# Regrouping the norm between the stages of a two-block transformer kernel, and a shorter prologue

## What is computed

```
def rms_norm(x, gain):
    xf = x.astype(jnp.float32)
    y = xf * lax.rsqrt(jnp.mean(xf * xf, axis=-1, keepdims=True) + EPS)
    return (y * gain.astype(jnp.float32)).astype(x.dtype)

def modulate(x, gain, shift, scale):
    return rms_norm(x, gain) * (1.0 + scale[:, None]) + shift[:, None]

    mod = cond @ ada_w[l] + ada_b[l]
    sh1, sc1, g1, sh2, sc2, g2, sh3, sc3, g3 = jnp.split(mod, N_MOD, axis=-1)
    h = modulate(x, norm_ffn1[l], sh1, sc1)
    x = x + 0.5 * (1.0 + g1)[:, None] * swiglu(h, ffn1_w1[l], ffn1_w3[l], ffn1_w2[l])
```

## Time and profile before

| | us |
|---|---|
| three runs | 3274.8, 3290.96, 3296.43 |
| median | 3290.96 |
| the profiled execution's own time | 3291.47 |
| its span, first to last instruction | 3289.7 |

### The profile page before, as it was taken

The page is one execution under the profiler, slowest core; times in us unless marked ns, Lnnn a source line. Parts: engine busy times, 40 slices in busy tenths (PEclk is TensorE's granted clock), DMA queues, the critical chain, the costliest instruction groups (busy, mean ns, idle before and its releaser), DMA issues.

```text
span 3289.7 us, 62648 instructions
## 1 busy us (share of the span) xinstructions
PE 3056.7 (93%) x24944; PEld 2881.9 (88%) x24944; DVE 2290.9 (70%) x3886; ACT 1374.4 (42%) x2129; POOL 239.7 (7%) x315
## 2 busy tenths in 40 slices
PE   1999987999999998889999998799899999999898
PEld 1999885899999997669999998699856899999798
DVE  6887564558867675555786888587957568676654
ACT  1445413444444452243444436443644444444332
POOL 1002001010000110000101000000023100100001
PEclk9999988899999998899999999899979899999899
DMA  7895401248967651015687884287400368676253
GB/s 293 308 332 184 136 2 64 91 166 294 335 227 276 218 172 46 19 61 185 230 309 253 313 310 159 90 309 285 160 1 26 129 240 318 244 262 234 95 188 122
DMA packets 172570, 631.99 MB, mean 192 GB/s; under 512 B 19152, under 2 KB 19408, under 8 KB 171856
## 3 DMA queue, kind: packets, MB, share of 16 engines
q1 hardware_dynamic: 123696, 450.88, 38.9%
q10 hardware_dynamic: 48672, 178.28, 15.6%
HBM read 628.04 MB, written 1.05 MB: 191 GB/s over the span
## 4 chain that ended last, share of the span: by engine, by line
PE 86%; DVE 10%; ACT 2%; DMA 1%; issue 1%; POOL 0%; DVEq 0%; SPq 0%; ACTq 0%
PE psum L531 23%; PE psum L533 22%; PE psum L532 22%; DVE w_lo L503 2%; DVE xl L1830 2%; PE psum L1985 2%; PE psum L1972 1%; PE psum L549 1%; PE psum L550 1%; DMA ada_w<-ada_dram 1%; PE psum L1987 1%; PE psum L649 1%; DVE bc L1830 1%; PE psum L555 1%; PE psum L1181 1%
## 5 line engine op out<-in xcount | busy, mean ns | idle before, releaser
L531 PE MATMUL psum<-h_hi,w_hi 128*128 128x256 f32 x4464 | 1251.4, 280 | 6.1 <-DVE h_lo L1724 4.6
L533 PE MATMUL psum<-h_lo,w_hi 128*128 128x256 f32 x4464 | 1248.4, 280 | 0.0
L532 PE MATMUL psum<-h_hi,w_lo 128*128 128x256 f32 x4464 | 1247.0, 279 | 0.0
L503 DVE TENSOR_TENSOR w_lo<-raw,w_hi 128x1024 fp32r<-128x1024 f32 x852 | 1041.3, 1228 | 181.5 <-ACT w_hi L490 180.4
L490 ACT ACTIVATE w_hi<-raw 128x1024 fp32r<-128x1024 f32 x852 | 873.4, 1054 | 408.6 <-DMA raw<-stream_dram 292.3
L531 PEld LDWEIGHTS psum<-h_hi,w_hi 128*128 128x128 f32 x4464 | 840.6, 188 | 16.3 <-issue 8.4
L532 PEld LDWEIGHTS psum<-h_hi,w_lo 128*128 128x128 f32 x4464 | 840.7, 188 | 0.0
L533 PEld LDWEIGHTS psum<-h_lo,w_hi 128*128 128x128 f32 x4464 | 840.4, 188 | 0.0
L532 PE MATMUL psum<-u_hi,w_lo 128*128 128x256 f32 x1584 | 448.3, 283 | 0.0
L531 PE MATMUL psum<-u_hi,w_hi 128*128 128x256 f32 x1584 | 448.2, 283 | 0.0
L533 PE MATMUL psum<-u_lo,w_hi 128*128 128x256 f32 x1584 | 448.2, 283 | 0.0
(11 more groups left out here) (357 smaller groups left out, 3617.4 us busy)
## 6 DMA issues: line engine op xcount, KB each, us to landing
raw<-stream_dram SPq DMA_DIRECT2D x852, 512.0 KB, 4.2
ada_w<-ada_dram ACTq DMA_DIRECT2D x328, 512.0 KB, 4.7
tmp<-c_dram ACTq DMA_DIRECT2D x8, 512.0 KB, 3.4
x<-x_dram SPq DMA_DIRECT2D x1, 1024.0 KB, 12.5
ctx_x<-ctx_dram ACTq DMA_DIRECT2D x1, 1024.0 KB, 5.4
means<-means_dram ACTq DMA_DIRECT2D x1, 1024.0 KB, 5.6
out_dram<-tmp SPq DMA_DIRECT2D x1, 1024.0 KB, 3.9
const<-const_dram SPq DMA_DIRECT2D x1, 848.5 KB, 8.8
```

The costliest lines, as they stand in the source:

```text
L503: p.nc.vector.tensor_tensor(p.w_lo[:, slot].rearrange("p k m -> p (k m)"), p.raw[:, slot], p.w_hi[:, slot].rearrange("p k m -> p (k m)").b ...
L531: mm(out, p.w_hi[:, slot, k], hi, start=start, stop=False, skip_group_check=skip)
L532: mm(out, p.w_lo[:, slot, k], hi, start=False, stop=False, skip_group_check=skip)
L533: return mm(out, p.w_hi[:, slot, k], lo, start=False, stop=stop, skip_group_check=skip)
```

## The change

- **Squares.** Where the norm follows an FFN, `gates`, `ssd_out` or `state` stage, GpSimd squares x[:, 0] to x[:, 6] and adds them into one tile, `sq_sum` (7 squares and 6 sums), in tiles 4 to 6 of `tmp`, without the wait for the modulation products. DVE squares x[:, 7] itself (`last_square`). PE sums two tiles (4 products) instead of eight.
- **Root.** ACT reads the sums from PSUM, applies scale and epsilon and takes the root in one instruction; a small Sqrt without a wait stands ahead of it (`table`). DVE then takes the reciprocal. The mean on DVE is gone.
- **Order on DVE.** `prep` and the first of the two splits move ahead of the update of x[:, 7] (`lead`), the second split moves behind h_lo. Norms 9 and 14 keep both behind the last update.
- **Prologue.** 16 modulation tiles instead of 28; the gate of the first FFN is formed inside that FFN (`late_gate`), which takes 56 tiles instead of 44. `c` has a buffer of its own and the first product no longer waits for the constants. Three units are split between the products, the first norm's sums and root run beside them. SP loads three units, then waits until 13 products are done, and loads the other five; most of the constants and `par2` come behind these.
- **Rope tables.** The 22 DVE instructions for the angles (`trig_vector`) move from the start into the first `project` stage, behind the split at t = 25; the two Sin instructions of ACT into the first `gdn` stage.
- **Fetches.** The loads of `ctx` and `means` move behind the norm that they stood ahead of.
- Several semaphores are merged, which changes no wait's place.

```diff
+SQ_STEPS = 2 * (KD - 1) - 1
+HEAD_SPLITS = (9, 11, 13)
...
     for c in range(SLOTS):
+        if c == len(HEAD_SPLITS):
+            sp.wait_ge(p.sem["ada_summed"], ADA_HEAD - 3)
         load(0, c)
+    for to, src in late:
+        sp.dma_start(to, src).then_inc(p.sem["tables_loaded"], 16)
...
-def head_scalar(p, act, st):
-    c_row_silu(p, act, st)
+def head_scalar(p, act, st, first):
+
+    act.wait_ge(p.sem["head_row_full"], 16)
+    p.nc.scalar.activation(p.head_row[:], p.head_row[:], ACT.Silu).then_inc(p.sem["head_row_ready"], 1)
     for s in range(st.ada_n):
         ada_load(p, act, s + ADA_SLOTS)
-
-
-def head_vector(p, dve, st):
-    dve.wait_ge(p.sem["c_row_ready"], 1)
+        if s == 10:
+            act.wait_ge(p.sem["tables_loaded"], 16)
+            root_scalar(p, act, first)
+        if s in HEAD_SPLITS:
+            split_hi(p, act, HEAD_SPLITS.index(s))
+
+
+def head_vector(p, dve, st, first):
+
+    dve.wait_ge(p.sem["head_row_ready"], 1)
     for s in range(st.ada_n):
-        ada_dot(p, dve, s)
+        ada_dot(p, dve, s, p.head_row[:])
+        if s == 5:
+            dve.wait_ge(p.sem["loaded"], p.n_loads)
+            last_square(p, dve, first)
+        if s == 12:
+            root_vector(p, dve, first)
+        if s in HEAD_SPLITS:
+            split_lo(p, dve, HEAD_SPLITS.index(s))
...
 def norm_gpsimd(p, pool, st):
 
-    a, x = st.at, st.x(p)
-    pool.wait_ge(p.sem["ada_summed"], a("ada_summed"))
+    a, x, mult = st.at, st.x(p), ALU.mult
+    if st.unit0 and not st.gathered:
+        pool.wait_ge(p.sem["ada_summed"], a("ada_summed"))
     if a("h_ready"):
         pool.wait_ge(p.sem["h_ready"], a("h_ready"))
     if st.on_ctx:
         pool.wait_ge(p.sem["fetched"], 16)
-    for m in range(KD):
+    step = a("sq_ready")
+    for m in range(KD - 1):
         if a("x_ready"):
             pool.wait_ge(p.sem["x_ready"], a("x_ready") - KD + m + 1)
-        p.nc.gpsimd.tensor_tensor(p.tmp[:, m], x[:, m], x[:, m], ALU.mult).then_inc(p.sem["sq_ready"], 1)
+        to = (p.sq_sum if m == 0 else p.sq_part[:, m % 2]) if st.gathered else p.tmp[:, m]
+        p.nc.gpsimd.tensor_tensor(to, x[:, m], x[:, m], mult).then_inc(p.sem["sq_ready"], 1)
+        step += 1
+        if st.gathered and m:
+            pool.wait_ge(p.sem["sq_ready"], step)
+            p.nc.gpsimd.tensor_tensor(p.sq_sum, p.sq_sum, to, ALU.add).then_inc(p.sem["sq_ready"], 1)
+            step += 1
+
+
+def last_square(p, dve, st):
+
+    a, x, m = st.at, st.x(p), KD - 1
+    if st.on_ctx:
+        dve.wait_ge(p.sem["fetched"], 16)
+    if st.unit0:
+        dve.wait_ge(p.sem["ada_summed"], a("ada_summed"))
+    if a("h_ready"):
+        dve.wait_ge(p.sem["h_ready"], a("h_ready"))
+    if a("x_ready"):
+        dve.wait_ge(p.sem["x_ready"], a("x_ready"))
+    p.nc.vector.tensor_tensor(p.tmp[:, m], x[:, m], x[:, m], ALU.mult).then_inc(p.sem["last_sq"], 1)
 
 
 def norm_tensor(p, pe, st):
 
     a, mm, ones = st.at, p.nc.tensor.matmul, p.c("ones")[:, 0:1]
-    for m in range(KD):
-        pe.wait_ge(p.sem["sq_ready"], a("sq_ready") + m + 1)
+    squares = [p.tmp[:, m] for m in range(KD - 1)]
+    if st.gathered:
+        squares = [p.sq_sum]
+        pe.wait_ge(p.sem["sq_ready"], a("sq_ready") + SQ_STEPS)
+    for m, sq in enumerate(squares + [p.tmp[:, KD - 1]]):
+        if m == len(squares):
+            pe.wait_ge(p.sem["last_sq"], a("last_sq") + 1)
+        elif not st.gathered:
+            pe.wait_ge(p.sem["sq_ready"], a("sq_ready") + m + 1)
         for c in range(2):
-            ins = mm(p.psum[:, 2, c : c + 1], p.tmp[:, m, c * P : c * P + P], ones, start=m == 0 and c == 0,
-                     stop=m == KD - 1, skip_group_check=True)
+            ins = mm(p.psum[:, 2, c : c + 1], sq[:, c * P : c * P + P], ones, start=m == 0 and c == 0,
+                     stop=m == len(squares), skip_group_check=True)
     ins.then_inc(p.sem["sum_done"], 1)
-    pe.wait_ge(p.sem["root_ready"], a("root_ready") + 1)
+    pe.wait_ge(p.sem["norm_step"], a("norm_step") + 1)
     for c in range(2):
         ins = mm(p.psum[:, 3, c * P : c * P + P], p.root[:, c : c + 1].to_broadcast([P, P]), p.c("ident"),
                  start=True, stop=True)
...
 def root_scalar(p, act, st):
-    act.wait_ge(p.sem["norm_step"], st.at("norm_step") + 2)
-    p.nc.scalar.activation(p.root[:], p.mean[:], ACT.Sqrt).then_inc(p.sem["root_ready"], 1)
+    p.nc.scalar.activation(p.table[:], p.c("eps"), ACT.Sqrt)
+    act.wait_ge(p.sem["sum_done"], st.at("sum_done") + 1)
+    p.nc.scalar.activation(p.mean[:], p.psum[:, 2, 0:2], ACT.Sqrt, bias=p.c("eps"), scale=1.0 / D).then_inc(
+        p.sem["root_ready"], 1)
 
 
 def root_vector(p, dve, st):
 
-    a, v = st.at, p.nc.vector
-    dve.wait_ge(p.sem["sum_done"], a("sum_done") + 1)
-    v.tensor_scalar(p.mean[:], p.psum[:, 2, 0:2], 1.0 / D, EPS, ALU.mult, ALU.add).then_inc(p.sem["norm_step"], 1)
-    dve.wait_ge(p.sem["norm_step"], a("norm_step") + 1)
-    v.reciprocal(p.mean[:], p.mean[:]).then_inc(p.sem["norm_step"], 1)
-    dve.wait_ge(p.sem["rinv_ready"], a("rinv_ready") + 1)
+    dve.wait_ge(p.sem["root_ready"], st.at("root_ready") + 1)
+    p.nc.vector.reciprocal(p.root[:], p.mean[:]).then_inc(p.sem["norm_step"], 1)
 
 
 def norm_scalar(p, act, st):
     a = st.at
-    for s in range(2):
-        split_hi(p, act, st.unit0 + AHEAD + s)
-    root_scalar(p, act, st)
+    if st.unit0:
+        split_hi(p, act, st.unit0 + AHEAD)
+        root_scalar(p, act, st)
     for m in range(KD):
         act.wait_ge(p.sem["scaled"], a("scaled") + m + 1)
         p.nc.scalar.activation(
             p.h_hi[:, m], p.tmp[:, m], ACT.Identity, bias=p.mod[:, 3 * st.n, m : m + 1]
         ).then_inc(p.sem["h_rounded"], 1)
+    for s in range(AHEAD + 1 if st.unit0 else len(HEAD_SPLITS), AHEAD + 2):
+        split_hi(p, act, st.unit0 + s)
+
+
+def lead(p, dve, st):
+
+    nxt = st.norm
+    if nxt.kind == "norm":
+        prep_vector(p, dve, nxt.prep)
+        split_lo(p, dve, nxt.unit0 + AHEAD)
+    nxt.led = True
 
 
 def norm_vector(p, dve, st):
     nc, a, x = p.nc, st.at, st.x(p)
-    if st.on_ctx:
-        dve.wait_ge(p.sem["fetched"], 16)
-    if st.unit0:
-        dve.wait_ge(p.sem["unit_done"], st.unit0)
-    for s in range(2):
-        split_lo(p, dve, st.unit0 + AHEAD + s)
-    root_vector(p, dve, st)
+    if not st.unit0:
+        prep_vector(p, dve, st.prep)
+    else:
+        last_square(p, dve, st)
+        if not st.led:
+            split_lo(p, dve, st.unit0 + AHEAD)
+            prep_vector(p, dve, st.prep)
+        root_vector(p, dve, st)
+    dve.wait_ge(p.sem["rinv_ready"], a("rinv_ready") + 1)
     for m in range(KD):
         nc.vector.scalar_tensor_tensor(
             p.tmp[:, m], x[:, m], p.mod_a[:, st.n, m : m + 1], p.psum[:, 3, 0:T], ALU.mult, ALU.mult
         ).then_inc(p.sem["scaled"], 1)
     for m in range(KD):
         norm_lo(p, dve, st, m)
+    for s in range(AHEAD + 1 if st.unit0 else len(HEAD_SPLITS), AHEAD + 2):
+        split_lo(p, dve, st.unit0 + s)
...
+        if j == 0 and st.late_gate:
+            late_gate(p, dve, st)
         for m, end in enumerate(ends):
             if j == min(end + 1, FT - 1):
+                if m == KD - 1:
+                    dots(2 * FT + j, 2 * FT + j + 1)
+                    lead(p, dve, st)
                 dve.wait_ge(p.sem["unit_done"], u0 + 2 * FT + end + 1)
                 nc.vector.scalar_tensor_tensor(
                     x[:, m], p.psum[:, 4 + m % 4, 0:T], p.mod_g[:, st.n, m : m + 1], x[:, m], ALU.mult, ALU.add
                 ).then_inc(p.sem["x_ready"], 1)
-        dots(2 * FT + j, 2 * FT + j + 1)
+        if j < FT - 1:
+            dots(2 * FT + j, 2 * FT + j + 1)
...
+        if t == 25 and st.layer == 0:
+            trig_vector(p, dve)
...
+        if gq and st.layer == 0:
+            trig_scalar(p, act)
...
+        if m == KD - 1:
+            lead(p, dve, st)
...
-ADA_HEAD = 28
+ADA_HEAD = 16
...
-    def branch(n, vec, tiles, which, n_vec=3, **more):
+    def branch(n, vec, tiles, which, n_vec=3, fetch=None, **more):
 
         nonlocal tile
-        add("prep", n=n, n_vec=n_vec, ada0=ADA_FIRST[which], **more)
+        late = not which and not n
+        add("prep", n=n, n_vec=2 if late else n_vec, ada0=ADA_FIRST[which], **more)
         add("norm", n=n, **more)
+        stages[-1].prep = stages[-2]
+        if fetch:
+            add("fetch", what=fetch, **more)
         if n != 1:
-            add("ffn", n=n, vec=vec, ada0=tile, ada_n=tiles, **more)
+            add("ffn", n=n, vec=vec, ada0=tile, ada_n=tiles, late_gate=late, ada_units=64 if late else ADA_UNITS, **more)
             tile += tiles
...
+    for at, st in enumerate(stages):
+        if st.kind in ("ffn", "gates", "ssd_out"):
+            st.norm = next(nxt for nxt in stages[at + 1 :] if nxt.kind != "prep")
+            st.norm.gathered = True
+        if st.kind == "state":
+            stages[at + 2].gathered = True
...
```

(18 more changed lines are left out.)

136 lines of the change are left out of this document (85 added, 51 removed).

## The result

| | before | after |
|---|---|---|
| first runs, median (lowest to highest) | 3283.4 of 4 (3274.8 to 3296.4) | 3196.0 of 4 (3191.9 to 3199.3) |
| ratio, with its 95% interval | | 0.9744 (0.9715 to 0.9773) |
| the profiled execution, its span | 3291.5, 3289.7 | 3193.4, 3191.6 |
| mean granted clock over the span | 0.946 | 0.956 |

The kernel is 87 us faster. One execution of x10 further down, 3253 us at a clock of 0.941 beside 3198 to 3207 for its others, is a slow one and stays out of its ratio.

The account below looks back on a forecast made before the run. PE was taken as the bound, busy for 93% of the span, so other engines' work counts only where PE waits. From 3291.5, 38.7 + 30.2 - 2 - 1.5 - 2 - 1 = 62.4 gives 3229 us, range 3209 to 3252.

Parts of the forecast that it names:

- Starting point: Whole kernel: savings were subtracted from the profiled execution, 3291.5 us, taken as 0.5 above the median of the runs.
- the table load: Norms: ACT's table for the root costs and saves nothing, as it was already loaded under the last products before.
- the clock and GpSimd: Norms: losses of 2 us for the low clock and 1 us for GpSimd's added instructions.
- Prologue: Before the first FFN: its first product starts at about 38.9 us instead of 77.6, 38.7 us saved.
- Back from the prologue: First FFN and first `project`: moved modulation products cost 2 us of PE waiting, moved angles 1.5 us.
- The rival of a starved FFN: First FFN: if only 310 GB/s can be kept up, loads make PE wait, total 3240 us; chance 0.12.
- The one wait for w_lo behind the angles: First `project` stage: PE waits 1.5 us (0 to 3) for a split delayed by the moved angles.
- Norms: Gaps between stages: 4.7 us behind a stage, 5.5 behind `gates`; 30.2 us saved together.
- The last x starts 0.8 us later: Norms behind `gates`: the early split and `prep` delay the last update of x by 0.8 us.
- Clock: Norms: the low clock stretch is expected at each, with 2 us of loss taken and 13 us as the bound.
- the rival of a clock that holds: Norms: some see no clock fall; six of twelve would save 13 us, total 3216; chance 0.06.
- The slower rival: Norms: the early split waits for a late load and holds the last x; kernel could end above 3291; chance 0.02.

Follow-up runs that it names:

- x10: The changed kernel with 96 bytes more per partition behind the new scalar, so that u_hi starts at 151552: 3203.7 us, ratio 0.9775.
- x17: x9 run once more, beside the changed kernel on one chip: 3226.2 us, ratio 0.9831.
- x9: The changed kernel with the new scalar put into another small tensor's free part, so that u_hi stays at 151424: 3230.8 us, ratio 0.9852.
- x5: The changed kernel with DVE's three prologue splits two products behind ACT's: 3192.0 us, ratio 0.9724.
- x4: The changed kernel with `prep` and the first split behind the last x at every norm: 3195.4 us, ratio 0.976.
- x6: The changed kernel with only the modulation early behind `gates`, both splits behind the norm there: 3188.8 us, ratio 0.971.
- x7: The changed kernel with 20 unused filler products (8, 4 and 8) in the norm gaps: 3195.5 us, ratio 0.975.

## Why the prediction was wrong, step by step

**Starting point.** This is the first step that failed. "From 3291.5 (the profiled execution, 0.5 above the median of the runs)": over the 61 runs on record, on several chips, the kernel before has a median of 3277, so the start was 14 us too high. The profiled execution had the long course of the `mix` stretch (347.9 us, where ten other traces have 330 to 332). Of the 61, seven lie at 3291 to 3296, those with a clock on record at 0.945 or 0.946, and all others at 3269 to 3283. The three runs that I had, 3275, 3291 and 3296, already showed two courses, and I didn't ask which one the profile was.

**No term at all.** This is the second. What lies behind `table` in memory had no term, and the length of the u products alone is 15 us of the time. The whole diff did show `table` in the middle of the allocations; the prediction speaks only of the table load, which "costs and saves nothing". From profile to profile 98.1 us went: 34.2 in the prologue, 32.5 at the norms, the pooling and the end, 17.5 in the FFNs (15 of them by that length), 18.0 in the `mix` stretch, less 4.0 that the other stretches are longer. The forecast had terms for the first two and for what they give back. So of the 33 us by which the time lies below it, 14 are the start and 15 the place; 2 of waiting in the first FFN that didn't come and 2.3 more at the norms stand against 4.5 less in the prologue, and the remaining 4 against the 3 that I had taken off for the clock and GpSimd.

The sum of the terms, 3229, stands beside 3226 and 3231 measured without the shift (x17, x9), but by luck: the start was 14 us too high, and the terms together 13 to 16 us too good.

**Prologue.** "1.5 for what ACT's three splits and its table hold back" was mis-sized: 4.9 us of DVE idle, and x5 takes 4.2 of them away. The landings were right (product 5 started at 16.47, forecast 16.5), and so 34.2 us were saved for 38.7 forecast.

**Back from the prologue.** "I take 2 us of PE waiting" in the first FFN: none, at 374 GB/s. The rival of a starved FFN falls, and the Trainium skill (HBM Reference, Specifications), by which it would not starve, was right in that; its 358 GB/s for a core's share is passed here by 4%, by one core alone. The one wait for w_lo behind the angles came as forecast, 1.5 us; x4 reads 0.7 there.

**Norms.** Right in sum (32.5 for 30.2), by two errors that cancel in part: a plain gap is 0.5 shorter, those behind `gates` 0.6 longer. "The last x starts 0.8 us later" was 1.2 (1.38 us behind PE's end, where x6 has 0.23), since `prep` took 1.4 us beside GpSimd instead of 0.8. The Trainium skill (SBUF — State Buffer, "Who interferes with whom") has the rule: a DVE instruction with two SBUF inputs excludes GpSimd's reads, and so does a tensor_scalar when it runs in a two-port mode. The rows agree (0.59 and 0.71 against 0.17), and I had applied it only to splits.

**Clock.** "A gap of 4.7 us is still longer than every one of those falls, so I expect the low stretch in each ... I take 2 us of loss." The stretch did come at each, so the rival of a clock that holds did not happen as I put it; but its length changed from 7 and 10.5 to 3.5 and 7, and instead of a loss the FFNs took 17.5 us less, 2 more than the shorter products give. The bound of this term, 13 us of low clock that moves from idle time under products, doesn't show behind the norms either, with u_hi at its old place: the gaps of norms 2 to 12 hold 40 us of low time before and 11 in x9 and in x17, and the nine FFNs took 1701.6 us before and 1699.0 and 1700.9 there. These two kernels gain 46 to 49 us in the medians, where the idle time that went is 34.2 + 32.5 = 66.7. Of the missing 18 to 20 the traces show 4 to 5 between norms 2 and 3 (457.7 us before, 462.4 and 461.4), 2 of them in the first `project` stage. A long course of the `mix` stretch would be another 11 to 13, if most executions of the kernel before have the short one; that is argued from their times, as no trace of such an execution is kept.

**The range.** The bounds that I named for the prologue and the norms give 3220 to 3241 around 3229, and not 3213 to 3247. None was for the start or the place, and no bound or rival holds 3196.

**The slower rival** (a split that holds the last x) did happen, where it had no price of mine: behind `gates`, 1.3 us twice.

## What to carry to other kernels

When a diff adds a tensor, however small, compare the addresses of everything behind it and the duration of products that the diff does not touch; pad back to the old place before crediting the edits. Before counting from one profile, ask with a few plain runs which of the kernel's courses it shows, and look at the granted clock stage by stage. Moving work ahead of a wait pays only if it ends before the wait does, beside whatever else runs there; and filler in a gap has to stand ahead of the wait that makes it.

## What the hardware did unexpectedly

- The same 4752 products took 283 ns with the moving operand u_hi at byte 151424 of a partition, 282 at 151552, 280 or 279 at 151456, 278 at 151488, with the weights `w_hi` at 49280; u_lo moved along with u_hi.
- In `mix`, where PE and DVE answer one another, the clock of the profiled execution before stayed at 1.2 GHz from 2404.6 us for 27 us, though the profile shows PE busy without a pause from 2405 to 2430 (12 to 14 products in 5 us, against 23 at the full clock right behind). Six of eighteen traces have such a second low stretch there, and take 9 to 18 us longer.
- An FFN without any low clock took 186.15 us at six places of x7 and 187.9 at two, with 88 and 87 products in 10 us. The products follow one another every 116.7 ns in the one kind and every 117.8 in the other. Nothing in the rows tells the two kinds apart.
- One core moved 376 GB/s for 20 us at a DMA share of 1.00.
